# Sending the samples' memory queries to all partitions by DMA, in place of products with the identity

## The chip, the core and the metric

One core of a Trainium2 chip runs the whole kernel in one launch. The metric is the device time in microseconds, the median of several executions. Engines: TensorE (PE) for products, VectorE (DVE), ScalarE (ACT), GpSimd (POOL), and SyncE (SP), which here only issues loads. Data lies in 128 partitions of on-chip memory (SBUF); products land in banks of PSUM.

## The reference

A decoder layer runs on two inputs at once: a prompt of 512 tokens and 8 samples of one token each. The part that matters is the memory attention:

```python
def mem_attend(h, mk, mv, w_xq, w_xo):
    q = (h @ w_xq).reshape(B, T, MEM_HEADS, MEM_HEAD_DIM)             # 4 heads of 256
    s = jnp.einsum('bthd,bmhd->bhtm', q, mk).astype(jnp.float32) * MEM_SCALE
    p = jax.nn.softmax(s, -1).astype(mv.dtype)
    o = jnp.einsum('bhtm,bmhd->bthd', p, mv).reshape(B, T, MEM_HEADS * MEM_HEAD_DIM)
    return o @ w_xo
```

For the prompt, keys and values are projected from 256 memory tokens (`mem @ w_mk`, `mem @ w_mv`). For the samples they come from a cache: each of the 8 samples has its own 256 keys and 256 values in every head, 1 MB of keys and 1 MB of values per sample.

## The kernel before

All activations are held transposed (features on partitions, 520 tokens along the row, in two halves of 260). Every large product is made from float32 values split in two parts, high and low: three matmuls (L1944 high by high, L1945, L1946) for each 128 x 128 block. A weight slot is loaded into `wraw` (two buffers), ScalarE writes its high part `whi` (L912), VectorE its low part `wlo` (L1394). The load queue may send slot s when VectorE has split slot s-2 (`load_w`, wait on `w_lo`), and ScalarE may overwrite a `whi` when TensorE is done with the slot three back.

The order of work is written out by hand on each engine, and each engine waits for semaphores. PSUM has a ring of seven banks: the list `bank_order` says in which order results take them.

Around the change the order is this. The query projection `xq` has 8 tiles (m = 0..7), two for each head. After m = 2, 4, 6 and 7, `query_rows(h)` turns the 8 sample columns of head h (kept in `qcs`) into 8 rows (L2320), and ScalarE scales them into `q_nat` (L928), 8 partitions x 256. A sample's scores need its 256 keys, which lie in `kv_slot` as 128 partitions x 2 keys; so the query of a sample and head has to stand in all 128 partitions. `spread(g)` makes that with the identity: a full float32 product of `q_nat` with one broadcast column of `ident` (L2329) fills half a bank for each (head, sample) pair. VectorE then multiplies and sums it against the two keys of each partition (`scores_of`, L1738, two products a pair), into `Sc`. The 32 pairs come in nine groups `SPREADS`, g0 to g8, each in two halves. A half is one bank.

Groups g0 to g3 follow xq tiles 3, 5, 6 and 7 on TensorE and VectorE. Groups g4 to g7 follow the first four tiles of the memory key projection (`key_tile(j)`, slots S_MEM to S_MEM+3, "mm"), on VectorE each behind the split of slot S_MEM+j+2. Then come the prompt's scores of head 0 (`mem_scores(0)`), their maxima on VectorE (L1785), g8, the maximum over the samples' scores (L1808), and on TensorE the first value tile (`value_tile(0)`, slots S_MEM+4 and S_MEM+5). The maximum goes through TensorE once (L2435), becomes a diagonal (L1815) and is spread by one product (L2439). Key tile 4 (slot S_MEM+6) stands ahead of that product, key tile 5 (S_MEM+7) behind it.

The cached keys and values share eight 1 MB slots. Keys 0 to 6 are loaded before and during the projections, key 7 when xq tile 7 is done. Values take over slots whose keys are spent: `K_SLOT` and `V_SLOT` give the slots, and the load queue waits for the score groups.

Of the kernel before, what the change touches and what calls it, by code (L numbers as in the profile page):

```python
# [81 lines left out]
SPREADS = [[[(0, 0), (0, 1)], [(0, 2)]], [[(1, 0), (1, 1)], [(1, 2)]],  # L82
# [4 lines left out]

K_SLOT, V_SLOT = [0, 1, 2, 3, 4, 5, 6, 7], [3, 5, 4, 6, 2, 7, 2, 7]
# [17 lines left out]
def bank_order():  # L106
# [37 lines left out]
    def spread(g):  # L144
        return [("qb", g, i) for i in (0, 1)]

# [9 lines left out]
    for m in range(KD):  # L156
        o += [("xq", m, f) for f in (0, 1)]
        if m == 0:
            o += [("ssq", "nx")]
        if m in (2, 4, 6):  # L160
            o += [("qt", m // 2 - 1)]
        if m in (3, 5, 6, 7):
            o += spread((3, 5, 6, 7).index(m))
    o += [("qt", 3)]
    for j in range(4):
        o += [("mm", j)] + spread(4 + j)
    o += mem_scores(0) + [("mn", 0)] + spread(8) + [("mv", 0), ("cmxt",), ("mm", 4), ("cmxb",), ("mm", 5)]
# [113 lines left out]
def build(nc, a, consts, outs):  # L281
# [4 lines left out]
    with ctx:  # L286
# [125 lines left out]
        q_by = q_diag[:, 0:NK * NB * G16].rearrange("p (x i h) -> p x i h", i=P // SQ, h=NH)  # L412
# [49 lines left out]
        q_nat = at("q_nat", [D], F32, o_rstd)  # L462
        prod = at("prod", [MD], F32, o_tmp)
# [8 lines left out]
        qcs = keep("qcs", [KD, NB])  # L472

# [67 lines left out]
        qcs_set = sem("qcs_set")  # L541
        stored = sem("stored")
# [148 lines left out]

        def cached(eng, n):
# [18 lines left out]
        def _(sp):  # L711
# [88 lines left out]
        def _(gp):  # L800
# [96 lines left out]
            gp.memset(Pv_pad[:, :], 0.0).then_inc(vpad_set, 1)  # L897
            squares("nf", "xo2", KD, lambda c: xT[:, c, :])
# [3 lines left out]
        def _(act):  # L902
# [1683 lines left out]
```

## Time and profile before

| | |
|---|---|
| three timed runs | 903.75 us median (900.0 to 905.21) |
| the profiled execution | 899.05 us, span 897.3 us |
| TensorE busy | 828.3 us (92%) |
| VectorE busy | 484.9 us (54%) |
| ScalarE busy | 327.2 us (36%) |
| GpSimd busy | 103.1 us (11%) |
| mean granted TensorE clock | 0.958 |
| moved by DMA | 102.57 MB, 114 GB/s over the span |

The profile gives each instruction with its line, what it writes and reads, and what ended the idle time of its engine ahead of it. Times are microseconds from the start of the span. "Clock" is the granted TensorE clock as a share of 2.4 GHz; 0.50 is 1.2 GHz. A matmul's duration in the timeline reaches into the next one, since they are pipelined; the distance between starts is what one costs. In L2329 one product is recorded twice.

### The profile page before, as it was taken

What the parts mean: (1) busy time and instruction counts of PE and PEld (TensorE: products, weight loads), DVE (VectorE), ACT (ScalarE), POOL (GpSimd) and SP (SyncE); (2) the same over time, 40 slices, a digit from 0 to 9 for tenths busy, and PEclk for the clock granted to TensorE, in tenths of its full rate; (3) what the DMA queues carried; (4) which work ended last, traced back from release to release, by engine and by line L of the source; (5) the groups of instructions that cost most, each with busy time, mean ns of one, the idle gap of its engine ahead of it and who ended that gap; (6) DMA issues with size and microseconds to landing.
All of it is one profiled execution on the core that took longest, in us unless ns stands there. A gap on an engine that the chain in (4) does not pass through costs nothing.

```text
span 897.3 us, 16200 instructions
## 1 busy us (share of the span) xinstructions
PE 828.3 (92%) x6599; PEld 788.0 (88%) x6599; DVE 484.9 (54%) x1055; ACT 327.2 (36%) x714; POOL 103.1 (11%) x143
## 2 busy tenths in 40 slices
PE   5989989877899999789999899999999999999994
PEld 4979978733799998689799899999999999999994
DVE  5577556584354457665555475555555555222322
ACT  5314676510342323355533343333333333112312
POOL 0366104020134000000035100000000000000000
PEclk8999998879799999889999999999999999999998
DMA  7412337040723714573623233333332232332312
GB/s 218 122 48 81 87 96 293 2 175 1 257 71 101 253 48 142 207 258 115 219 72 95 71 94 95 94 95 95 95 92 86 87 91 88 109 110 83 88 42 95
DMA packets 133792, 102.57 MB, mean 114 GB/s; under 512 B 8567, under 2 KB 127280, under 8 KB 130639
## 3 DMA queue, kind: packets, MB, share of 16 engines
q1 hardware_dynamic: 128231, 87.17, 31.7%
q0 software_dynamic: 1792, 10.49, 3.0%
q10 hardware_dynamic: 3696, 3.88, 1.3%
q8 instruction: 52, 0.85, 0.4%
q14 instruction: 21, 0.17, 0.1%
HBM read 96.59 MB, written 5.17 MB: 113 GB/s over the span
## 4 chain that ended last, share of the span: by engine, by line
PE 77%; DVE 6%; ACT 4%; DMA 3%; issue 2%; SPq 0%; ACTq 0%; DVEq 0%
PE ps L1944 23%; PE ps L1946 23%; PE ps L1945 23%; DMA wraw<-in_w_mk_dram 2%; DVE turned_c L1667 1%; PE ps L2281 1%; PE ps L2421 1%; DVE prod L1738 1%; DMA kv_slot<-in_cache_mem_v_dram 1%; PE ps L2376 1%; PE ps L2377 1%; PE ps L2378 1%; PE ps L2329 1%; DVE turned_r L1668 1%; PE ps L2253 0%
## 5 line engine op out<-in xcount | busy, mean ns | idle before, releaser
L1944 PE MATMUL ps<-B_hi,whi 128*128 128x260 f32 x992 | 283.4, 286 | 9.9 <-DVE wlo L1394 4.3
L1946 PE MATMUL ps<-B_hi,wlo 128*128 128x260 f32 x992 | 281.4, 284 | 0.0
L1945 PE MATMUL ps<-B_lo,whi 128*128 128x260 f32 x992 | 281.2, 283 | 0.0
L1394 DVE TENSOR_TENSOR wlo<-wraw,whi 128x512 fp32r<-128x512 f32 (+1 forms) x250 | 170.2, 723 | 167.1 <-ACT whi L912 164.8
L912 ACT ACTIVATE whi<-wraw 128x512 fp32r<-128x512 f32 (+1 forms) x250 | 140.3, 610 | 201.8 <-PE ps L1946 159.2
L1944 PEld LDWEIGHTS ps<-B_hi,whi 128*128 128x128 f32 x992 | 187.9, 189 | 11.9 <-issue 9.3
L1946 PEld LDWEIGHTS ps<-B_hi,wlo 128*128 128x128 f32 x992 | 188.3, 190 | 0.0
L1945 PEld LDWEIGHTS ps<-B_lo,whi 128*128 128x128 f32 x992 | 188.1, 190 | 0.1
L1945 PE MATMUL ps<-h_lo,whi 128*128 128x260 f32 x352 | 99.7, 283 | 0.0
L1946 PE MATMUL ps<-h_hi,wlo 128*128 128x260 f32 x352 | 99.4, 282 | 0.0
L1944 PE MATMUL ps<-h_hi,whi 128*128 128x260 f32 x352 | 99.4, 282 | 0.0
L1944 PE MATMUL ps<-A_hi,whi 128*128 128x260 f32 x264 | 76.2, 289 | 1.6 <-DVE A_lo L1394 1.2
L1946 PE MATMUL ps<-A_hi,wlo 128*128 128x260 f32 x264 | 75.7, 287 | 0.0
L1945 PE MATMUL ps<-A_lo,whi 128*128 128x260 f32 x264 | 75.6, 286 | 0.0
L1944 PEld LDWEIGHTS ps<-h_hi,whi 128*128 128x128 f32 x352 | 66.3, 188 | 0.0
L1946 PEld LDWEIGHTS ps<-h_hi,wlo 128*128 128x128 f32 x352 | 66.3, 188 | 0.0
L1945 PEld LDWEIGHTS ps<-h_lo,whi 128*128 128x128 f32 x352 | 66.2, 188 | 0.0
L1944 PEld LDWEIGHTS ps<-A_hi,whi 128*128 128x128 f32 x264 | 51.1, 193 | 2.1 <-DVE A_lo L1394 1.6
L1945 PEld LDWEIGHTS ps<-A_lo,whi 128*128 128x128 f32 x264 | 51.0, 193 | 0.1
L1946 PEld LDWEIGHTS ps<-A_hi,wlo 128*128 128x128 f32 x264 | 50.9, 193 | 0.0
L1424 DVE TENSOR_TENSOR xT<-ps,xT 128x260 f32<-128x260 f32 x48 | 20.4, 426 | 55.8 <-PE ps L1946 54.7
L918 ACT ACTIVATE h_hi<-hv 128x260 fp32r<-128x260 f32 x44 | 18.6, 422 | 71.9 <-DVE hv L1876 71.9
(405 smaller groups left out, 1286.4 us busy)
## 6 DMA issues: line engine op xcount, KB each, us to landing
wraw<-in_w_gate_dram SPq DMA_DIRECT2D x22, 512.0 KB, 3.8
wraw<-in_w_up_dram SPq DMA_DIRECT2D x22, 512.0 KB, 3.8
kv_slot<-in_cache_mem_k_dram SPq DMA_DIRECT2D x8, 1024.0 KB, 9.3
kv_slot<-in_cache_mem_v_dram SPq DMA_DIRECT2D x8, 1024.0 KB, 6.9
wraw<-in_w_down_dram SPq DMA_DIRECT2D x16, 512.0 KB, 4.0
wraw<-in_w_in_dram SPq DMA_DIRECT2D x9, 512.0 KB, 4.1
wraw<-in_w_out_dram SPq DMA_DIRECT2D x8, 512.0 KB, 4.1
wraw<-in_w_xq_dram SPq DMA_DIRECT2D x8, 512.0 KB, 5.2
```

The source lines that it names most:

```text
L912: act.activation(whi[:, s % SPL, c0:c1], wraw[:, s % RAW, c0:c1], ACT.Copy).then_inc(w_hi, 1)
L918: act.activation(dst, src, ACT.Copy, scale=scale).then_inc(hi, 1)
L1394: return dve.tensor_tensor(dst, src, high.bitcast(F32), ALU.subtract)
L1424: ins = dve.tensor_tensor(xT[:, m, c0:c1], b[:, 0:TH], xT[:, m, c0:c1], ALU.add)
L1667: dve.transpose(turned_c[:, b % 2].rearrange("p j k t -> p (j k t)"), past_c[b].rearrange("p j r -> p (j r)"))
L1668: value(("turned", b), dve.transpose(turned_r[:, b % 2].rearrange("p j k t -> p (j k t)"), past_r[b].rearrange("p j r -> p (j r)")))
L1738: ins = dve.tensor_tensor_reduce(prod[:, :], keys[:, m2, h * MD:(h + 1) * MD], q[:, n * MD:(n + 1) * MD], 1.0, 0.0, ALU.mult, ALU.add, Sc[ ...
L1944: pe.matmul(dst, left[0], right[0], start=first, stop=False)
L1945: pe.matmul(dst, left[0], right[1], start=False, stop=False)
L1946: return pe.matmul(dst, left[1], right[0], start=False, stop=last)
L2281: ins = pe.matmul(accO[strip, 0:KVL], P_pad[:, c:c + SQ], past_c[b][:, j, :], start=(b == 0 and 0 < j < 4), stop=(b == NB - 1 and j >= 4), ...
L2329: ins = pe.matmul(b[:, n * MD:(n + 1) * MD], ident[0:NB, sample:sample + 1].to_broadcast([NB, P]), q_nat[0:NB, h * MD:(h + 1) * MD], start ...
```

## The change

The queries reach the 128 partitions by DMA. ScalarE still scales the 8 rows of a head into `q_nat`, which now has two buffers; it then waits for its own result and stores the rows (8 x 1 KB) into a tensor `q_rows` in device memory. GpSimd issues, for each half group, one load that reads one or two rows and writes them to all 128 partitions, 128 KB for each pair, into one of four buffers `q_by`. It waits for the store of the heads involved and, from the fifth half on, for VectorE to have spent the half four places back (`q_spent`). VectorE's products read `q_by` in place of PSUM. The `spread` products and their 18 places in the ring of banks are gone.

The order of the groups changes too. They follow xq tiles 4 to 7 (before 3, 5, 6, 7), and their members are others: g4 now has three pairs and g7 three, g5 and g6 four. Keys 4 and 5 swap slots, and the load queue waits for other groups at other places.

```diff
-SPREADS = [[[(0, 0), (0, 1)], [(0, 2)]], [[(1, 0), (1, 1)], [(1, 2)]],
-           [[(0, 3), (0, 4)], [(0, 5), (0, 6)]], [[(2, 0), (2, 1)], [(2, 2)]],
...
+SPREADS = [[[(0, 0), (0, 1)], [(0, 2)]], [[(0, 3), (0, 4)], [(0, 5), (0, 6)]],
+           [[(1, 0), (1, 1)], [(1, 2)]], [[(1, 3), (1, 4)], [(1, 5), (1, 6)]],
+           [[(2, 0), (2, 1)], [(2, 2)]], [[(2, 3), (2, 4)], [(3, 3), (3, 4)]],
+           [[(2, 5), (2, 6)], [(3, 5), (3, 6)]], [[(3, 0), (3, 1)], [(3, 2)]],
            [[(0, 7), (1, 7)], [(2, 7), (3, 7)]]]
-K_SLOT, V_SLOT = [0, 1, 2, 3, 4, 5, 6, 7], [3, 5, 4, 6, 2, 7, 2, 7]
+QBUF = 4
+K_SLOT, V_SLOT = [0, 1, 2, 3, 5, 4, 6, 7], [3, 5, 4, 6, 2, 7, 2, 7]
...
+        q_by = [at(f"q_by{i}", [2, MD], F32, o) for i, o in enumerate((o_rstd + 2048, o_rstd + 4096, o_tmp, take(2048)))]
+        q_rows = nc.dram_tensor("q_rows", [NH, NB, MD], F32, kind="Internal").ap()
...
             for i in range(2, len(MEM_TILES) + 2):
                 load_w(S_MEM + i)
-                if i == 5:
-                    freed(sp, ("qb", 7, 1))
-                if 5 <= i < 9:
-                    load_kv(NB + i - 5)
-                if i == 10:
-                    load_kv(NB + 4)
-                    freed(sp, ("qb", 8, 1))
-                if i == 11:
-                    load_kv(NB + 5)
+                if i in (4, 6, 8, 9):
+                    spent(sp, {4: 5, 6: 6, 8: 7, 9: 8}[i], 1)
+                for b in {4: (0,), 5: (1,), 6: (2,), 7: (3,), 9: (4,), 10: (5,)}.get(i, ()):
+                    load_kv(NB + b)
...
+            for g, halves in enumerate(SPREADS):
+                for i, members in enumerate(halves):
+                    n = 2 * g + i
+                    for h, _ in members:
+                        gp.wait_ge(q_out[h], 16)
+                    if n >= QBUF:
+                        gp.wait_ge(q_spent, n - QBUF + 1)
...
+                    gp.dma_start(q_by[n % QBUF][:, 0:len(members), :], rows.rearrange("h b d -> (h b) d").unsqueeze(0)
+                                 .to_broadcast([P, len(members), MD])).then_inc(q_in[n % QBUF], 16)
...
+                freed(act, ("qt", h))
+                act.dma_start(q_rows[h], q_nat[0:NB, h % 2, :]).then_inc(q_out[h], 16)
...
                 for i, members in enumerate(SPREADS[g]):
-                    q = full(dve, ("qb", g, i))
+                    slot_ = (2 * g + i) % QBUF
+                    dve.wait_ge(q_in[slot_], 16 * ((2 * g + i) // QBUF + 1))
...
-                                prod[:, :], keys[:, m2, h * MD:(h + 1) * MD], q[:, n * MD:(n + 1) * MD],
+                                prod[:, :], keys[:, m2, h * MD:(h + 1) * MD], q_by[slot_][:, n, :],
...
-                if m in (3, 5, 6, 7):
-                    scores_of((3, 5, 6, 7).index(m))
+                if m >= 4:
+                    scores_of(m - 4)
...
-            def spread(g):
...
-                        ins = pe.matmul(b[:, n * MD:(n + 1) * MD], ident[0:NB, sample:sample + 1].to_broadcast([NB, P]),
-                                        q_nat[0:NB, h * MD:(h + 1) * MD], start=True, stop=True)
...
             for j in range(4):
                 key_tile(j)
-                spread(4 + j)
             mem_scores(0)
             key_rows(0)
-            spread(8)
```

On TensorE, at the end of the last xq tile, these instructions stood before (the last product of the tile, group g3 of three pairs, the turn of head 3, the first products of key tile 0):

```order
L1946 MATMUL ps<-B_hi,wlo 128x260
L2329 MATMUL ps<-q_nat,ident 128x256 [waits bank_free6,lo]
L2329 MATMUL ps<-q_nat,ident 128x256 [waits bank_free6]
L2329 MATMUL ps<-q_nat,ident 128x256 [waits bank_free6,lo]
L2320 MATMUL ps<-ident,qcs 8x128 [waits qcs_set,bank_free6]
L2320 MATMUL ps<-ident,qcs 8x128
L1944 MATMUL ps<-mT_hi,whi 128x256 [waits bank_free0,w_lo,lo]
```

and these stand there now:

```order
L1963 MATMUL ps<-B_hi,wlo 128x260
L2337 MATMUL ps<-ident,qcs 8x128 [waits qcs_set,lo]
L2337 MATMUL ps<-ident,qcs 8x128
L1961 MATMUL ps<-mT_hi,whi 128x256 [waits lo,w_lo]
L1962 MATMUL ps<-mT_lo,whi 128x256
```

The three products of the group are gone, and with them the waits for their banks; the same holds after xq tiles 3, 5 and 6, after key tiles 0 to 3 and after the key rows of head 0.

On the load queue (SP), from the load of key 7 on, before (`in_w_mk` are key tiles, `in_w_mv` halves of a value tile, `in_cache_mem_v` cached values; `bank_free4` there is the release of group g7):

```order
L754 DMA kv_slot7_180<-in_cache_mem_k_dram 128x2048 [waits bank_full3]
L719 DMA wraw_50<-in_w_mk_dram 128x8x128 [waits w_lo] x2
L719 DMA wraw_50<-in_w_mv_dram 128x4x256 [waits w_lo] x2
L754 DMA kv_slot3_176<-in_cache_mem_v_dram 128x2048 [waits bank_free4]
L719 DMA wraw_50<-in_w_mk_dram 128x8x128 [waits w_lo]
L754 DMA kv_slot5_178<-in_cache_mem_v_dram 128x2048
L719 DMA wraw_50<-in_w_mk_dram 128x8x128 [waits w_lo]
L754 DMA kv_slot4_177<-in_cache_mem_v_dram 128x2048
L719 DMA wraw_50<-in_w_mv_dram 128x4x256 [waits w_lo]
L754 DMA kv_slot6_179<-in_cache_mem_v_dram 128x2048
```

and now (the first `q_spent` is for group g5, the second for g6):

```order
L759 DMA kv_slot7_180<-in_cache_mem_k_dram 128x2048 [waits bank_full4]
L724 DMA wraw_50<-in_w_mk_dram 128x8x128 [waits w_lo] x2
L724 DMA wraw_50<-in_w_mv_dram 128x4x256 [waits w_lo]
L759 DMA kv_slot3_176<-in_cache_mem_v_dram 128x2048 [waits q_spent]
L724 DMA wraw_50<-in_w_mv_dram 128x4x256 [waits w_lo]
L759 DMA kv_slot5_178<-in_cache_mem_v_dram 128x2048
L724 DMA wraw_50<-in_w_mk_dram 128x8x128 [waits w_lo]
L759 DMA kv_slot4_177<-in_cache_mem_v_dram 128x2048 [waits q_spent]
L724 DMA wraw_50<-in_w_mk_dram 128x8x128 [waits w_lo]
L759 DMA kv_slot6_179<-in_cache_mem_v_dram 128x2048
```

The first cached values moved one weight load forward: they and their wait for scores now stand ahead of the second half of value tile 0 (slot S_MEM+5). The wait itself is for g5, where it was for g7.

## Rows read from the trace of the kernel before

**Rows 1.** Busy PE, PEld, DVE, ACT, POOL (records) in stretches, clock, DMA share, GB/s.
```profile
310.94:371.92 60.98, 60.98 (x435) 55.10 (x434) 43.41 (x162) 20.29 (x46) 0.00 (x0) 1.00 0.29 88
341.45:344.45 3.00, 3.00 (x26) 2.86 (x24) 2.14 (x10) 0.47 (x1) 0.00 (x0) 1.00 0.89 343
377.45:382.09 4.64, 4.64 (x24) 4.44 (x24) 1.15 (x2) 1.81 (x4) 0.00 (x0) 0.63 1.08 397
382.09:385.14 3.05, 0.00 (x1) 0.03 (x1) 2.71 (x7) 1.18 (x3) 0.00 (x0) 0.87 1.01 398
385.67:390.96 5.29, 5.29 (x25) 5.29 (x25) 2.55 (x6) 1.85 (x5) 0.00 (x0) 0.50 0.91 316
```

**Rows 2.** One line, L2329: min/median/max ns, first and last start us.
```profile
L2329 PE MATMUL ps<-q_nat,ident x64: 374/374/477, 310.9 to 365.9; 8*128 8x256 f32 x64
```

**Rows 3.** Timeline of TensorE: start us, us, instruction; two half groups, the matmul behind.
```profile
310.94 1.56 PE L2329 MATMUL ps<-q_nat,ident 8*128 8x256 f32 x6
312.43 0.39 PE L1944 MATMUL ps<-B_hi,whi 128*128 128x260 f32 x1
...
331.96 1.99 PE L2329 MATMUL ps<-q_nat,ident 8*128 8x256 f32 x8
333.88 0.39 PE L1944 MATMUL ps<-B_hi,whi 128*128 128x260 f32 x1
```

**Rows 4.** Timeline of the load queue (SP): start us, us spent issuing, transfer.
```profile
339.93 0.34 SPq L754 DMA_DIRECT2D kv_slot<-in_cache_mem_k_dram  x1
...
348.81 5.61 SPq L719 DMA_DIRECT2D wraw<-in_w_mv_dram  x2
...
367.54 0.34 SPq L754 DMA_DIRECT2D kv_slot<-in_cache_mem_v_dram  x1
367.93 0.42 SPq L719 DMA_DIRECT2D wraw<-in_w_mk_dram  x1
```

**Rows 5.** Timeline of ScalarE: first use of two weight loads, idle time before.
```profile
346.75 1.16 ACT L912 ACTIVATE whi<-wraw 128x512 fp32r<-128x512 f32 x2 [4.49 <-DMA wraw<-in_w_mk_dram]
...
375.44 1.15 ACT L912 ACTIVATE whi<-wraw 128x512 fp32r<-128x512 f32 x2 [3.46 <-DMA wraw<-in_w_mk_dram]
```

**Rows 6.** Chain of waits in order of time: start us, us, what.
```profile
369.02 11.24 DMA wraw<-in_w_mk_dram
```

**Rows 7.** Timeline of VectorE: splits of w2 to w5, maxima and end of scores, splits w6, w7.
```profile
347.48 1.30 DVE L1394 TENSOR_TENSOR wlo<-wraw,whi 128x512 fp32r<-128x512 f32 x2 [3.75 <-ACT whi L912]
...
352.73 1.29 DVE L1394 TENSOR_TENSOR wlo<-wraw,whi 128x512 fp32r<-128x512 f32 x2
...
357.98 1.29 DVE L1394 TENSOR_TENSOR wlo<-wraw,whi 128x512 fp32r<-128x512 f32 x2
...
362.30 1.29 DVE L1394 TENSOR_TENSOR wlo<-wraw,whi 128x512 fp32r<-128x512 f32 x2
...
367.54 1.42 DVE L1785 TENSOR_REDUCE cstat<-ps 128x2 f32<-128x512 f32 x2
...
372.82 0.22 DVE L1808 TENSOR_REDUCE cols<-Sc 128x32 f32<-128x64 f32 x1
...
376.10 1.29 DVE L1394 TENSOR_TENSOR wlo<-wraw,whi 128x512 fp32r<-128x512 f32 x2 [3.06 <-ACT whi L912]
...
380.94 1.29 DVE L1394 TENSOR_TENSOR wlo<-wraw,whi 128x512 fp32r<-128x512 f32 x2 [3.55 <-ACT whi L912]
```

**Rows 8.** VectorE by tile: min/median/max ns, first and last start us; operands, shapes.
```profile
L1738 DVE CUSTOM_DVE_ANT_0 prod<-kv_slot,ps x64: 413/420/424, 312.1 to 372.4; 128x256 f32<-128x256 f32 x64
...
L1394 DVE TENSOR_TENSOR mk_lo<-kv_T,mk_hi x8: 417/422/428, 348.7 to 412.5; 128x256 fp32r<-128x256 f32 x8
...
L1394 DVE TENSOR_TENSOR kl<-kr,kk x4: 744/1190/1287, 58.4 to 62.1; 64x260 fp32r<-64x260 f32 x2, 64x252 fp32r<-64x252 f32 x2
```

**Rows 9.** POOL's own issue in ns; time to landing of the cached key and value loads.
```profile
L892 POOL DMA_INDIRECT past_c<-in_cache_kv_latent_dram,row_ids x8: 940/943/1173, 136.6 to 187.0; - x8
...
DMA to landing us min/median/max: 4.9/8.2/13.0
```

More of the change, by code:

```diff
@@ L143, in bank_order @@
             o += [("mt", k) for k in range(4)]
-    def spread(g):
-        return [("qb", g, i) for i in (0, 1)]
     def mem_scores(h):
@@ L541, in build @@
         qcs_set = sem("qcs_set")
+        q_out = [sem(f"q_out{h}") for h in range(NH)]
+        q_in = [sem(f"q_in{i}") for i in range(QBUF)]
+        q_spent = sem("q_spent")
         stored = sem("stored")
@@ L690, in build, with spent @@
             kv_count.append(seen[i])
+        def spent(eng, g, i):
+            eng.wait_ge(q_spent, 2 * g + i + 1)
         def cached(eng, n):
@@ L897, in _ @@
             gp.memset(Pv_pad[:, :], 0.0).then_inc(vpad_set, 1)
+            full(gp, ("ssq", "nx"))
+            for g, halves in enumerate(SPREADS):
[5 more added lines that the diff above has]
+                        gp.wait_ge(q_spent, n - QBUF + 1)
+                    (h0, b0_), (h1, b1_) = members[0], members[-1]
+                    rows = q_rows[h0:h0 + 1, b0_:b1_ + 1, :] if h0 == h1 else q_rows[h0:h1 + 1, b0_:b0_ + 1, :]
+                    gp.dma_start(q_by[n % QBUF][:, 0:len(members), :], rows.rearrange("h b d -> (h b) d").unsqueeze(0)
+                                 .to_broadcast([P, len(members), MD])).then_inc(q_in[n % QBUF], 16)
             squares("nf", "xo2", KD, lambda c: xT[:, c, :])
@@ L1151, in _ @@
                 group = slice(SQ * i, SQ * (i + 1))
-                ins = act.activation(q_by[group, :, i, :], x[group, 0:NK * NB * NH].rearrange("p (x h) -> p x h", h=NH), ACT.Copy)
+                ins = act.activation(q_diag_by[group, :, i, :], x[group, 0:NK * NB * NH].rearrange("p (x h) -> p x h", h=NH), ACT.Copy)
                 if i < P // SQ - 1:
@@ L1250, in value_tile @@
                 if h == 0:
-                    freed(act, ("qb", 6, 1))
+                    spent(act, 7, 1)
                 else:
@@ L1276, in turned @@
                     if h == 0 and mb == 0:
-                        freed(act, ("qb", 6, 1))
+                        spent(act, 7, 1)
                     high(("cpt", h, mb), PTc_hi[:, mb, :], b)
@@ L1742, in scores_of @@
                                 step(ins)
-                    frees(ins, ("qb", g, i))
-                    freed(dve, ("qb", g, i))
+                    ins.then_inc(q_spent, 1)
+                    spent(dve, g, i)
             for m in range(KD):
@@ L2321, in query_rows @@
                 filled(ins, ("qt", h))
-            def spread(g):
-                for i, members in enumerate(SPREADS[g]):
-                    b = out(("qb", g, i))
-                    for n, (h, sample) in enumerate(members):
-                        freed(pe, ("qt", h))
-                        ins = pe.matmul(b[:, n * MD:(n + 1) * MD], ident[0:NB, sample:sample + 1].to_broadcast([NB, P]),
-                                        q_nat[0:NB, h * MD:(h + 1) * MD], start=True, stop=True)
-                    filled(ins, ("qb", g, i))
             for m in range(KD):
@@ L2346, in _ @@
                     query_rows(m // 2 - 1)
-                if m in (3, 5, 6, 7):
-                    spread((3, 5, 6, 7).index(m))
             query_rows(3)
```

16 lines of the change are left out of this document (8 added, 8 removed), and 2 rows, old and new, of the table SPREADS.

## The prediction

> **What bounds the kernel now.** I began with the granted clock and the engine table, which say that TensorE is busy in 92% of the span, and then cut the memory attention into stretches. From 310.94 to 371.92 us TensorE is never idle [rows 1]. Part of that work is what the change deletes: the 64 recorded passes of L2329, the spreading products [rows 2]. The order of TensorE shows that they stand in its way: a half group of three samples pushes the next matmul from 310.94 to 312.43, a group of four from 331.96 to 333.88 [rows 3], that is 1.49 and 1.92 us. Over nine groups (four of three samples, five of four) this is 4 x 1.49 + 5 x 1.92 = 15.6 us.
>
> That is not yet the gain. The chain of waits from 347 to 385 us does not run through those products. It runs through VectorE's score products, the load queue that waits for them, and a weight load of 11.24 us [rows 6]. VectorE has no idle time from 347.48 until its last score at 372.82 [rows 7]. TensorE then stands still: mk tile 4 begins at 377.45 and runs at a mean granted clock of 0.63, nothing runs from 382.09 to 385.14, and mk tile 5 takes 5.29 us at clock 0.50 (1.2 GHz), where mk tile 0 took 3.00 at full clock [rows 1]. So there are three limits in a row: TensorE to the end of the query projection, VectorE through the scores, late loads behind them. I price each in turn.
>
> Names: w2 to w7 are the loads of the memory projection's slots S_MEM+2 to S_MEM+7 (w2, w3 and w6, w7 for mk tiles 2, 3 and 4, 5; w4, w5 the halves of value tile 0). v0 to v5 are the loads of cached values. g4 to g8 are the last five score groups.
>
> **Step 1: TensorE up to the end of the query projection.** Groups g0, g1 and g2 of before stand ahead of xq tile 7: 1.49 + 1.49 + 1.92 = 4.90 us. With them gone, tile 7 ends at 339.93 - 4.90 = 335.0. Nothing else is late there: in the new order an xq tile with four samples costs VectorE what a key tile with four does, 5.25 us, and one low part more (0.42 [rows 8]), less than the 6.0 us of TensorE (48 matmuls, 24 in 3.00 [rows 1]). (The 5.25: a split and low part with four samples takes 352.73 - 347.48 = 5.25, one with three 362.30 - 357.98 = 4.32 [rows 7]; one sample, two products, is 0.93.) The remaining 10.7 us of products lie beside VectorE's work, and I count them as nothing.
>
> **Step 2: w2 still waits for tile 7.** The queue sends key load 7 at 339.93 when tile 7 ends, then w2 and w3 [rows 4]. w2 is in at 346.75, and VectorE splits it at 347.48 [rows 5, 7], 7.55 us behind the end of tile 7. This is not touched, so the split comes at 342.6. But now two broadcasts (256 KB each, g5's) share the engines. At the 343 GB/s of that stretch [rows 1] one of them costs 0.75 us; I add 0.7 for one and get 343.3.
>
> **Step 3: VectorE's chain, and a load that was put behind a wait.** From the split of w2: g4 now has three samples (4.32), g5 has four (5.25), so g5 is spent at 352.9. Here the order of the load queue hurts. Before, w5 left with the pair at 348.81, ahead of the wait for the scores [rows 4]. Now v0 stands ahead of w5, and v0 waits for g5. What this looks like was seen later in the old trace: v0 at 367.54, w6 at 367.93, and w6 in use by ScalarE at 375.44 [rows 4, 5], 7.9 us after v0. Add 0.9 us for g7's broadcasts (384 KB at about 0.4 MB per us [rows 1]): w5 is in at 361.7 and its VectorE split begins 0.66 later (376.10 - 375.44), at 362.4. VectorE is ready at 352.9 + 5.25 = 358.1, so it waits 4.3 us. Then split and g7 (4.32) to 366.7; the maxima of score tile 0 and g8, as before 372.82 - 367.54 = 5.28 [rows 7], to 372.0. Before this was 372.82. Nearly the whole lead is used up at this point.
>
> **Step 4: the loads behind the scores are early.** Before, w6 and w7 were ordered only after 367.54 and came late: VectorE waited 3.06 and 3.55 us for them [rows 7]. Now w6 leaves at about 354 and w7 at about 364, as soon as their buffers are split, and w7 even with its old 11.24 us is needed only at 372.8 plus ScalarE's exponentials; with four 1 MB loads spread over 15 us instead of crowded into 3 I take it to be in by 370. mk tile 4 starts 1.35 us after the split of w6 (377.45 - 376.10), at 372.0 + 0.2 + 1.35 = 373.55, 3.9 us earlier. I leave it its 4.64 us, since TensorE idles about as long ahead of it: end 378.2. VectorE's path to the diagonal (second split to release of TensorE 385.14 - 380.94 = 4.2, plus 1.2 for the first split) would be ready at 377.6, so the idle 3.05 us vanish. mk tile 5 starts 0.53 later, at 378.7 against 385.67: 7.0 us earlier. Since TensorE now runs through, as it had from 377.45 when its clock came back, I take tile 5 at 3.07 instead of 5.29 us: 2.2 more.
>
> **The sum.** 7.0 + 2.2 = 9.2 us, from 391 us on a pure shift: the remaining stages have the same work and loads with the same distances. The profiled execution took 899.05 us with a span of 897.3; less 9.2 it is 889.9. The three timed runs have a median of 903.75, 4.7 above it, so I forecast 894.5 for a median.
>
> **Costs that no row shows.** The round trip (8 KB to device memory, then a broadcast to 128 partitions): the nearest rows are cached loads of 1 MB, which land in 4.9 to 13.0 us [rows 9]; POOL's own issue takes 0.94 [rows 9]. A broadcast smaller by four to eight times should be near the low end, 5 us with the issue. What it may take: buffers turn after four halves; g6's first half is ordered when g4's first is spent (346.7) and needed at 354.4, 7.7 us later, and if it is late it eats only into the 4.3 us wait for w5. g7 and g8 have 12 us. So up to about 12 us the trip costs nothing. The four stores cost ScalarE half a microsecond each, beside tiles for which it waits. POOL has nothing behind them but the squares for the last norm, far later.
>
> The product from SBUF instead of PSUM: 420 ns with one operand in PSUM; a 256-column subtraction with both operands in SBUF takes 422 [rows 8]. I take it as unchanged, with 0.05 us per product (1.8 us over 36) to either side. The Trainium skill, "VectorE: DVE Perf Modes", section on the TRN2 errata, gives a fixed part of 120 cycles from PSUM and 58 from SBUF, which would make each product 65 ns shorter and the last 36 of them 2.3 us; these rows show no such difference, so the sum goes without it.
>
> Two SBUF operands can also collide with POOL: the four kl subtractions took 1.19 us in the median instead of 0.42 [rows 8], which I put down to POOL's tensor work beside them. If an issue of 0.94 us stopped VectorE wholly, the two that fall ahead of g5's end would cost 1.9 us; the lower bound is zero, and I take zero, the issue being no tensor work. The Trainium skill, "SBUF — State Buffer", section "Who interferes with whom", says that two-input operations contend only with GpSimd's reads of SBUF, and infers that writing descriptors needs the write side; the kl rows fit the first, no row here tests the second.
>
> **Rivals.** (A) The forecast, 7 to 11.5 us gained. (B) w5 is not late: v0 goes out slowly enough or bandwidth suffices, as for w5 before, whose split at 357.98 waited for nothing [rows 7]. The 4.3 us come back; mk tile 4 could start at 369.3 and tile 5 at 374.4: gain 13.5, time 890.2. For it speaks that the engines are idle at 358 us in the old trace; against it, that the same order of loads gave 7.9 us there. (C) The gain is mostly lost: broadcasts of 12 to 13 us, or the freed time is handed to later waits (TensorE waits once for the v7 load near 443 us, and values could crowd weights again), or tile 5 stays at 1.2 GHz and w6 or w7 come late too, 11.24 us after their turn. Gain 0 to 4.5, time about 901. (D) The broadcast replaces the product as the bound. Every fourth half waits for a trip of L: from g0's first half spent (319.5) four trips lead to g8: g8 begins at 319.5 + 4L + 3 x 1.86. The gain is gone when g8's end comes at 381.2, which is L = 13.1 us, just over the slowest load of this trace; at L = 15 the kernel is 4 x 1.9 = 7.6 us slower, 911.4. It would need each small broadcast, through POOL's queue, to be slower than the slowest 1 MB load. Against: those loads queued behind each other.
>
> **How the numbers follow.** A 0.58, B 0.12, C 0.20, D 0.10. A difference of 0.5% (4.5 us) is about what a measurement of this kernel can tell from none. Faster: A, B and 0.06 of C, 0.76. Same: the rest of C, 0.14. Slower: D, 0.10. The timed runs spread over 5 us, so the range must be wider than A's own (892 to 897): from just beyond B, 888.5, into C at 901.5; what lies outside is D, a part of C and a little above B.
>
> **What would show it.** Right: no TensorE record in L2329's place; tile 7 ends near 335; VectorE idles some 4 us for a w_mv weight near 358 us, ahead of g7; no idle time on it for a q_by broadcast; the last score near 372, almost unmoved; mk tile 5 near 379 at clock 1.00, and from there the old trace shifted by about 9. Step 3 is wrong if VectorE does not wait for w5 (then B), or waits for q_in (C, D); step 4 if mk tile 4 waits for w_mk as before. The forecast is wrong as a whole if the stage ends earlier and the kernel does not.

## The result and the profile after

The changed kernel took 893.68 us in the median of five runs (892.82 to 894.52), the kernel before 903.75 beside it: ratio 0.9893, 95% interval 0.9867 to 0.9919. That is 10.1 us less, where 9.2 were forecast. The profiled execution took 892.82 us, span 890.9.

The two traces cannot be laid on each other by their absolute times. These rows are the first matmul of xq tile 0 and the first product with w_xo, of before, of the changed kernel, and of the changed kernel run again later, unedited:

```profile
286.45 0.36 PE L1944 MATMUL ps<-B_hi,whi 128*128 128x260 f32 x1 [0.96 <-issue]
450.26 0.39 PE L1944 MATMUL ps<-A_hi,whi 128*128 128x260 f32 x1 [0.64 <-DVE A_lo L1394]
```
```profile
290.88 0.36 PE L1961 MATMUL ps<-B_hi,whi 128*128 128x260 f32 x1 [0.96 <-issue]
443.95 0.39 PE L1961 MATMUL ps<-A_hi,whi 128*128 128x260 f32 x1 [0.64 <-DVE A_lo L1410]
```
```profile
283.45 0.36 PE L1961 MATMUL ps<-B_hi,whi 128*128 128x260 f32 x1 [0.96 <-issue]
437.28 0.39 PE L1961 MATMUL ps<-A_hi,whi 128*128 128x260 f32 x1 [0.64 <-DVE A_lo L1410]
```

The reader is to see that the stage is entered at 290.88 us in one trace and 283.45 in the other of the same program. Every time below is therefore counted from xq tile 0. "Forecast" is the prediction's own number less 286.45.

| from xq tile 0, us | before | forecast | after | after, again |
|---|---|---|---|---|
| end of xq tile 7 | 53.5 | 48.6 | 48.0 | 48.0 |
| split of w2 | 61.0 | 56.9 | 55.5 | 55.6 |
| split of w5 | 75.9 | 76.0 | 74.3 | 74.5 |
| end of the scores | 86.4 | 85.6 | 83.9 | 84.1 |
| mk tile 4 begins | 91.0 | 87.1 | 85.6 | 85.8 |
| mk tile 5 begins | 99.2 | 92.3 | 91.4 | 91.7 |
| prompt scores of head 1 | 104.5 | 95.3 | 94.3 | 94.7 |
| first product with w_xo ("the stage") | 163.8 | 154.6 | 153.1 | 153.8 |
| end of the span | 610.9 | 601.7 | 600.0 | 599.2 |

VectorE after, the splits of w2, w5, w6, w7 and the end of the scores, which answer to [rows 7]:

```profile
346.42 1.29 DVE L1410 TENSOR_TENSOR wlo<-wraw,whi 128x512 fp32r<-128x512 f32 x2 [2.93 <-ACT whi L924]
...
365.13 1.29 DVE L1410 TENSOR_TENSOR wlo<-wraw,whi 128x512 fp32r<-128x512 f32 x2 [3.84 <-ACT whi L924]
...
374.78 0.22 DVE L1825 TENSOR_REDUCE cols<-Sc 128x32 f32<-128x64 f32 x1
...
375.10 1.29 DVE L1410 TENSOR_TENSOR wlo<-wraw,whi 128x512 fp32r<-128x512 f32 x2
...
377.76 1.29 DVE L1410 TENSOR_TENSOR wlo<-wraw,whi 128x512 fp32r<-128x512 f32 x2 [1.36 <-ACT whi L924]
```

The wait for w5 is there, 3.84 us. The two waits of 3.06 and 3.55 us for w6 and w7 have become none and 1.36. The load queue after, which answers to [rows 4]:

```profile
338.89 0.34 SPq L759 DMA_DIRECT2D kv_slot<-in_cache_mem_k_dram  x1
...
356.04 0.34 SPq L759 DMA_DIRECT2D kv_slot<-in_cache_mem_v_dram  x1
356.81 0.37 SPq L724 DMA_DIRECT2D wraw<-in_w_mv_dram  x1
...
366.45 0.37 SPq L724 DMA_DIRECT2D wraw<-in_w_mk_dram  x1
```

v0 leaves at 356.04, w5 at 356.81, and w7 only at 366.45, when w5's split at 365.13 has freed its buffer. Before, w5 had left ahead of every cached value and had come into use 3.57 us later (these two lines are of before):

```profile
354.05 0.37 SPq L719 DMA_DIRECT2D wraw<-in_w_mv_dram  x1
357.62 1.15 ACT L912 ACTIVATE whi<-wraw 128x512 fp32r<-128x512 f32 x2 [2.35 <-DMA wraw<-in_w_mv_dram]
```

Now ScalarE uses w5 7.59 us behind its issue and 8.36 us behind v0, and w7 10.65 us behind its issue:

```profile
364.40 1.15 ACT L924 ACTIVATE whi<-wraw 128x512 fp32r<-128x512 f32 x2 [10.53 <-DMA wraw<-in_w_mv_dram]
...
377.10 1.15 ACT L924 ACTIVATE whi<-wraw 128x512 fp32r<-128x512 f32 x2 [1.50 <-DMA wraw<-in_w_mk_dram]
```

mk tiles 4 and 5 (the columns are those of [rows 1]); the last column but two is the clock:

```profile
376.45:381.70 5.25, 5.25 (x24) 5.04 (x24) 3.60 (x7) 2.26 (x5) 0.00 (x0) 0.54 0.99 357
382.26:385.35 3.09, 3.09 (x27) 3.09 (x27) 2.21 (x6) 2.21 (x6) 0.00 (x0) 1.00 0.95 380
```

The 3.05 us of idleness between them are now 0.25 (the product of the diagonal starts at 381.96, its input is made from 381.58 to 381.81). Tile 5 runs at full clock, tile 4 at nearly half. Ahead of tile 4 TensorE had stood idle for 5.13, 3.53 and 0.94 us, together 9.60, where before it had stood for 1.27 and 4.00:

```profile
366.48 0.58 PE L2381 MATMUL ps<-whi,mT_hi 128*128 128x256 f32 x1 [5.13 <-DVE wlo L1410]
...
375.14 0.37 PE L2438 MATMUL ps<-ident,cols 128*32 128x128 f32 x1 [3.53 <-DVE cols L1825]
```

The broadcasts and the products that read them:

```profile
L1755 DVE CUSTOM_DVE_ANT_0 prod<-kv_slot,q_by x64: 414/424/428, 322.1 to 374.3; 128x256 f32<-128x256 f32 x64
L908 POOL DMA_DIRECT2D q_by<-q_rows x18: 537/539/726, 312.6 to 361.9; - x18
...
who waited for it (us, times):
busy tenths in 40 slices 0000000000000046500000000000000000000000
DMA to landing us min/median/max: 3.1/3.9/9.2
```

Nobody waited for a broadcast: the line "who waited for it" has nothing under it, and VectorE has no idle time of any label ahead of a product that reads `q_by`.

### The profile page after: what moved, and what is told of

The parts are those of the page before. It is cut to its first block, busy times and chain, and to the rows that moved or that the text cites. A ratio compares the mean times of both kernels' runs of the same rounds, so it can differ in the third digit from the quotient of the medians.

```text
span 890.9 us, 16093 instructions
## 1 busy us (share of the span) xinstructions
PE 813.9 (91%) x6535; PEld 776.5 (87%) x6535; DVE 484.5 (54%) x1055; ACT 326.9 (37%) x714; POOL 113.2 (13%) x161
## 4 chain that ended last, share of the span: by engine, by line
PE 77%; DVE 6%; DMA 4%; ACT 3%; issue 2%; another core or an unknown queue 0%; SPq 0%; ACTq 0%; DVEq 0%
PE ps L1961 23%; PE ps L1963 23%; PE ps L1962 23%; DMA wraw<-in_w_mk_dram 2%; DVE turned_c L1683 2%; PE ps L2298 1%; DMA wraw<-in_w_mv_dram 1%; PE ps L2426 1%; PE ps L2381 1%; PE ps L2383 1%; PE ps L2382 1%; DMA kv_slot<-in_cache_mem_v_dram 1%; DVE turned_r L1684 1%; PE ps L2247 1%
## 5 line engine op out<-in xcount | busy, mean ns | idle before, releaser
L1962 PEld LDWEIGHTS ps<-h_lo,whi 128*128 128x128 f32 x352 | 66.2, 188 | 0.0
```

The source lines that it names most:

```text
L1962: pe.matmul(dst, left[0], right[1], start=False, stop=False)
```

## The experiments

All later runs were made beside new runs of the kernel before, which took 896.4 to 897.0 us in the median there, 0.8% less than in the first comparison. So ratios are compared, not times, and beside the ratios the stage (from xq tile 0 to the first product with w_xo), which came to 153.1 and 153.8 us in the two traces of one kernel, while the entry into it ranged from 282.7 to 290.9 us over all fourteen traces. "Rest" is from that product to the end of the span: the same work in every kernel, and yet it ranges over 3.3 us, and over 1.6 us in the two traces of one kernel. Stage and rest come from one trace of each kernel (two of the changed one), so a difference in the stage of less than about 1 us shows nothing, and the ratios, with their intervals of about 2 us to either side, show only the large ones.

| kernel | ratio (95%) | stage | rest |
|---|---|---|---|
| before | 1 | 163.8 | 447.0 |
| changed, first | 0.9893 (0.9867 to 0.9919) | 153.1 | 446.9 |
| changed, again | 0.9878 (0.9853 to 0.9902) | 153.8 | 445.3 |
| DMA queries, old groups and loads | 0.9978 (0.9960 to 0.9996) | 161.3 | 448.5 |
| products, new groups and loads | 0.9919 (0.9892 to 0.9945) | 155.8 | 448.5 |
| w5 ahead of v0 | 0.9892 (0.9872 to 0.9912) | 151.6 | 448.4 |
| w2 and w3 ahead of key 7 | 0.9878 (0.9857 to 0.9900) | 151.8 | 446.9 |
| both | 0.9845 (0.9819 to 0.9870) | 149.8 | 446.9 |
| both, g8 apart | 0.9868 (0.9845 to 0.9890) | 149.4 | 447.0 |
| the same, w7 ahead of v2 and v3 | 0.9877 (0.9853 to 0.9900) | 150.4 | 447.0 |
| the same, TensorE filled | 0.9860 (0.9840 to 0.9879) | 149.2 | 446.6 |
| DMA queries, old groups and loads, g5's broadcasts held | 0.9971 (0.9952 to 0.9991) | 161.3 | 448.6 |
| DMA queries, old groups, w2 and w3 ahead | 0.9912 (0.9892 to 0.9932) | 156.4 | 447.0 |
| changed, two buffers | 0.9982 (0.9962 to 1.0001) | 163.9 | 447.0 |

**The changed kernel again.**

> The changed kernel itself, unedited, on the chip of the runs beside it, as their common measure and to see what of its profile is its own. Theory: where it enters the memory attention (first matmul of xq tile 0 at 290.88 us in the first profile, 286.45 in that of before) is chance, since nothing ahead of it differs; the entry moves by some microseconds here, and the stretch from there to the prompt scores of head 1 stays at 94.3 us (before 104.5). The ratio to before is again 0.987 to 0.992. Rival: the entry is again 4 us late, so something of the change acts upstream.

Measured: entry at 283.45 us, 3.0 earlier than before where it had been 4.4 later; to the scores of head 1 94.7; ratio 0.9878. The theory holds: the entry moves from run to run of one program, and the change has no part in it.

**One half alone: the DMA.** The changed kernel with before's `SPREADS`, slots and load order (one of its places):

```diff
-                if m >= 4:
-                    scores_of(m - 4)
+                if m in (3, 5, 6, 7):
+                    scores_of((3, 5, 6, 7).index(m))
```

> One half of the change alone: the queries go by DMA, but groups, members, slots and load order are those of before (groups behind xq tiles 3, 5, 6, 7; v0 behind w5 and g7; four buffers). Theory (the two halves add up): the 4.9 us of products ahead of the end of xq tile 7 go, all behind it shifts by that, w5 is not late, but w6 and w7 come late as before (VectorE waits about 3 us for each, mk tile 5 at half clock): 4.5 to 5 us gained, 899 us (ratio 0.9945). Rival (the new load order carries the whole gain, and the freed TensorE time goes into waits for the same loads): 0 to 1 us gained, 903. A second rival, that this half carries all of it: 894.

**The other half alone: groups and loads.** The kernel before with the new `SPREADS`, slots and load order; the products stay (one of its places):

```diff
-                if m in (3, 5, 6, 7):
-                    spread((3, 5, 6, 7).index(m))
+                if m >= 4:
+                    spread(m - 4)
```

> The other half alone: the spreading products stay on TensorE, but groups, members, slots and load order are those of the changed kernel. Theory (the halves add up): tile 7 ends as late as before (4.9 us of products ahead of it), w5 comes late behind v0 (VectorE idle about 4 us), w6 and w7 are in early, mk tile 5 at full clock: 4 to 5 us gained, 899 us (ratio 0.995). Rival: without the freed time the late w5 eats up what w6 and w7 give, and the time is that of before, 902 to 904, or worse.

The DMA half shortens the stage by 2.5 us, the order half by 8.0; together 10.5, where the changed kernel has 10.7 and 10.0. They do add up, but not as expected (about 5 each). The ratios say the same within their intervals: 2.0 and 7.3 us. The products removed, 15.6 us of TensorE's time, are worth 2.5 us. The order half holds three things, the groups, the slots of the keys and the places of the loads; they were not tried apart.

Where the DMA half loses its lead, VectorE shows at the split of w2:

```profile
341.62 1.29 DVE L1415 TENSOR_TENSOR wlo<-wraw,whi 128x512 fp32r<-128x512 f32 x2 [6.39 <-ACT whi L929]
```

xq tile 7 ended at 330.69 us, 48.0 after tile 0, 5.5 sooner than before. But w2 is split 10.9 us behind it, not 7.55, so 2.1 us of the lead are left. (Ahead of that, with g1 still behind xq tile 5, VectorE also stood 2.05 us for a broadcast at 322.04, which it does not in the changed kernel; TensorE did not wait for it.) Around the tile's end GpSimd issued broadcasts (start, us, instruction):

```profile
327.35 1.06 POOL L913 DMA_DIRECT2D q_by<-q_rows  x2 [7.95 <-DMA q_rows<-q_nat]
329.18 0.54 POOL L913 DMA_DIRECT2D q_by<-q_rows  x1 [0.76 <-DVE Sc L1760]
331.04 0.54 POOL L913 DMA_DIRECT2D q_by<-q_rows  x1 [1.33 <-DVE Sc L1760]
334.85 0.54 POOL L913 DMA_DIRECT2D q_by<-q_rows  x1 [3.27 <-DVE Sc L1760]
335.79 0.54 POOL L913 DMA_DIRECT2D q_by<-q_rows  x1 [0.40 <-issue]
```

I took the last four, 1 MB, for the cause and held back the last two:

```diff
                         gp.wait_ge(q_out[h], 16)
+                    if n == 10:
+                        gp.wait_ge(w_loaded[(S_MEM + 2) % RAW], landed[S_MEM + 2])
                     if n >= QBUF:
                         gp.wait_ge(q_spent, n - QBUF + 1)
```

> The half change with DMA queries and the old groups and loads, and GpSimd holds the broadcasts of g5 until w2 has landed. In that half change 1 MB of broadcasts (g4 and g5) was ordered between 329 and 336 us, around the end of xq tile 7 at 330.7, and w2 came into use 10.2 us after the end of tile 7 where the changed kernel took 6.8; it gained 2.3 us of the 5.5 that the deleted products give there. Theory (the broadcasts crowd w2): with half of them held back w2 is in use 8.2 to 9 us after tile 7's end, and the stretch from xq tile 0 to the scores of head 1 shortens by 1 to 2 us. Rival (something else delays w2, key load 7 or the store of the query rows): still 10 us, nothing gained.

The split came 10.35 us behind the tile in place of 10.93, the first use of w2 9.62 in place of 10.20, and the stage did not move. The expectation failed: the two broadcasts ordered behind w2 cost it about 0.6 us, in one trace of each. And VectorE then stood 2.00 us for the last half of g8, whose broadcast was ordered at 358.23 and landed some 10 us later, where without the hold that wait was 0.57:

```profile
368.38 0.43 DVE L1762 CUSTOM_DVE_ANT_0 prod<-kv_slot,q_by 128x256 f32<-128x256 f32 x1 [2.00 <-issue]
```

What delayed w2 by the rest, the broadcasts ordered ahead of key 7 or something else, was not separated. Whether the wait for w2 is on the path of this half was then tried directly:

```diff
+            load_w(S_MEM + 2)
+            load_w(S_MEM + 3)
             full(sp, ("xq", KD - 1, 1))
             load_kv(7)
-            for i in range(2, len(MEM_TILES) + 2):
+            for i in range(4, len(MEM_TILES) + 2):
```

> The half change with DMA queries and the old groups and loads, with one edit: w2 and w3 go out ahead of key load 7, as tried on the changed kernel. Measured by the stretch from xq tile 0 to the first product with w_xo (before 163.8 us, this half change 161.3, the other half 155.8, the changed kernel 153.1 and 153.8). Theory (in this half VectorE's 6.39 us for w2 ate what the deleted products gave at the end of tile 7): the wait goes and the stretch falls by 4 to 6.4 us, to 155 to 157. Rival (the late w6 and w7 behind the scores hold the stage, w2 is covered): it stays above 160.

156.4 us, as expected: the 6.39 us wait is gone, and the stage is 7.5 us shorter than before instead of 2.5. The waits for w6 and w7 were left as they were (2.90 and 3.45). This is not the worth of the products with w2 repaired: the kernel before, in which VectorE stands 3.75 us for w2 [rows 7], was not run with w2 ahead.

**Why the order half gives more.** In it mk tile 4 took 3.10 us at full clock; in the changed kernel 5.25 at 0.54:

```profile
375.41:378.51 3.10, 3.10 (x24) 2.89 (x24) 2.96 (x5) 1.15 (x3) 0.00 (x0) 1.00 0.60 176
```

TensorE's longest pause ahead of that tile was 1.55 us there, against 5.13 and 3.53. The products between key tiles fill the waits; that such filling raises the clock is shown on another kernel below. Counting: mk tile 4 begins 1.6 us sooner than before, takes 1.5 less (4.64), the pause behind it is 0.79 in place of 3.05, and tile 5 runs at full clock: with that, 8.0 by the scores of head 1 (96.5 against 104.5). Against the changed kernel, tile 4 begins 3.8 us later (89.4 against 85.6), and 2.15 of that come back in the tile itself. VectorE's wait for w5 was shorter too, 2.23 us in place of 3.84:

```profile
364.11 1.29 DVE L1389 TENSOR_TENSOR wlo<-wraw,whi 128x512 fp32r<-128x512 f32 x2 [2.23 <-ACT whi L907]
```

**The two waits of the changed kernel.** First w5, step 3 of the prediction (rival B's condition, brought about):

```diff
-                if i in (4, 6, 8, 9):
-                    spent(sp, {4: 5, 6: 6, 8: 7, 9: 8}[i], 1)
-                for b in {4: (0,), 5: (1,), 6: (2,), 7: (3,), 9: (4,), 10: (5,)}.get(i, ()):
+                if i == 6:
+                    load_kv(NB + 1)
+                if i in (5, 6, 8, 9):
+                    spent(sp, {5: 5, 6: 6, 8: 7, 9: 8}[i], 1)
+                for b in {5: (0,), 6: (2,), 7: (3,), 9: (4,), 10: (5,)}.get(i, ()):
```

> The changed kernel with one edit: w5, the second weight load of value tile 0, goes out ahead of the wait for group g5 and of v0 (order now w4, w5, [g5] v0, w6, v1, [g6] v2, w7). Theory (step 3: the late w5 is on the path): in the changed kernel VectorE idles 3.84 us for it and TensorE 5.13. That VectorE wait falls under 0.5 us, the last score comes 3 to 4 us sooner after xq tile 0, and the kernel takes about 890 us, 3.5 below the changed kernel (ratio to before 0.985). Rival (the stage is held by the next loads anyway): the wait moves to w6 or w7, which now stand behind v0 and v1, and the time stays at 893 to 894 (0.989).

VectorE in this kernel, the split of w5 and group g8:

```profile
356.46 1.29 DVE L1412 TENSOR_TENSOR wlo<-wraw,whi 128x512 fp32r<-128x512 f32 x2
...
363.18 0.43 DVE L1757 CUSTOM_DVE_ANT_0 prod<-kv_slot,q_by 128x256 f32<-128x256 f32 x1 [0.75 <-DMA q_by<-q_rows]
...
367.16 0.42 DVE L1757 CUSTOM_DVE_ANT_0 prod<-kv_slot,q_by 128x256 f32<-128x256 f32 x1 [2.14 <-issue]
```

The split waits for nothing, 3.65 us sooner after xq tile 0 than in the changed kernel. But now VectorE waits twice for a broadcast. The second wait is labelled "issue"; the last broadcast says what it is. It was issued at 356.99, behind v0, w6, v1 and v2, and the landing times of the last two broadcasts (window 355 to 358 us) are:

```profile
DMA to landing us min/median/max: 8.0/9.0/10.1
```

356.99 + 10.1 = 367.1. Of 3.84 us 2.9 turned into that wait. Such a broadcast now had 7.3 and 8.0 us from its issue until VectorE was ready for it; in the changed kernel, with 3.84 us of waiting in front, g8's two had about 11. The end of the scores came 0.7 us sooner, the stage is 1.8 shorter than the mean of the changed kernel's two, and of that the ratio shows nothing (the rest of this trace is 448.4). Neither theory was right: the rival named w6 and w7.

Second w2, step 2 (the diff is the one above):

> The changed kernel with one edit: w2 and w3 go out ahead of the wait for the end of xq tile 7 and of key load 7; everything else keeps its order. Theory (step 2: the 7.55 us from the end of tile 7 to the split of w2 stand on the path of VectorE): the split of w2 comes within 2 us of the end of tile 7 in place of 7.56, the waits of TensorE for w2 and w3 (1.93 and 1.35 us) go, all of the chain behind shifts by 5 to 6.5 us, the kernel takes about 888 us (ratio 0.982). Rival (the chain is held by v0 and w5 or by key 7, which land when they did): gain under 1.5 us, 892 to 894.

```profile
340.11 1.29 DVE L1412 TENSOR_TENSOR wlo<-wraw,whi 128x512 fp32r<-128x512 f32 x2
...
360.00 1.29 DVE L1412 TENSOR_TENSOR wlo<-wraw,whi 128x512 fp32r<-128x512 f32 x2 [4.00 <-ACT whi L926]
```

The split comes 4.7 us behind tile 7 (335.44), not within 2: VectorE itself is busy with g3 until then. Of the 7.55 us only the 2.93 of waiting were to be had. The expectation of 5 to 6.5 us failed; VectorE also stood 0.93 us for a broadcast of g4. The stage is 1.7 us shorter.

> The changed kernel with both edits tried apart: w2 and w3 ahead of key load 7, and w5 ahead of v0. Alone each took 1.4 to 1.8 us off the stretch from xq tile 0 to the prompt scores of head 1 (94.31 us in the changed kernel, 92.54 and 92.91). Theory X (with both gone, the broadcasts of g8, which land behind the cached values, are the wait, as in the first edit, where VectorE stood 0.75 and 2.14 us for them): these waits grow to 3 to 5 us together, the stretch is 91 to 92.5 us, kernel 2 to 3 us below the changed kernel. Theory Y (the gains add): no such growth, the stretch is 89 to 91 us, kernel 4 to 5 us below.

Stage 149.8, 3.7 us under the mean of the changed kernel's two, which is about the sum of the two gains (1.8 and 1.7); 91.2 us to the scores of head 1. VectorE waited 0.56 and 2.92 us for g8's broadcasts. These waits and the 91.2 us lie in theory X, at its lower end; that the gains add is what theory Y said. The two theories were too close for one trace to part them. The median is 1.0 us below the changed kernel's, less than either said. The ratio is the lowest of all, but its interval overlaps those of most others.

**g8's broadcasts apart.** They get two buffers of their own, and wait for the end of the last xq tile in place of a spent half. The part that orders them:

```diff
-            for g, halves in enumerate(SPREADS):
-                for i, members in enumerate(halves):
-                    n = 2 * g + i
+            for n in list(range(14)) + [16, 17, 14, 15]:
+                for members in (SPREADS[n // 2][n % 2],):
```

> As the last one, and the two broadcasts of g8 have buffers of their own and are ordered ahead of those of g7, so they go out before the cached values. Theory X (g8's broadcasts are what held the last): VectorE waits for no q_by, the last score comes 3 to 5 us sooner than in the kernel with both edits, the stretch is 87.5 to 90 us and the kernel 2 to 4 us below that one, the fastest of all: ratio to before 0.981 to 0.985. Rival: w6 and w7, ordered behind the same values, or the exponentials and value tile, take over as the wait; under 1 us gained.

```profile
355.24 0.43 DVE L1763 CUSTOM_DVE_ANT_0 prod<-kv_slot,q_by 128x256 f32<-128x256 f32 x1 [1.79 <-DMA q_by<-q_rows]
...
366.67 1.29 DVE L1418 TENSOR_TENSOR wlo<-wraw,whi 128x512 fp32r<-128x512 f32 x2 [1.70 <-ACT whi L932]
```

The wait moved to g7, now ordered behind them, and w7 is late by 1.70. The end of the scores came 1.2 us sooner (79.8 after xq tile 0), the stage is 0.4 shorter, within the spread of one kernel's traces. The rival was right.

**w7, and TensorE's clock.**

```diff
-                if i in (5, 6, 8, 9):
-                    spent(sp, {5: 5, 6: 6, 8: 7, 9: 8}[i], 1)
-                for b in {5: (0,), 6: (2,), 7: (3,), 9: (4,), 10: (5,)}.get(i, ()):
+                if i in (5, 7, 8, 9):
+                    spent(sp, {5: 5, 7: 6, 8: 7, 9: 8}[i], 1)
+                for b in {5: (0,), 7: (2, 3), 9: (4,), 10: (5,)}.get(i, ()):
```

> The kernel with w2, w3 and w5 early and g8's own buffers, with w7 also ahead of v2 and v3. There w7 took 11.9 us from issue to use and VectorE stood 1.70 us for it; TensorE ran mk tile 4 at half clock (5.49 us) after 7.45 us of idleness, and ended it as late as the diagonal came. Theory: the wait for w7 goes, but mk tile 4 at half clock holds the place: 0.3 to 0.8 us gained of 1.7, stretch 148.6 to 149.2 (149.4 there). Rival: the full 1.7, 147.7.

The wait for w7 went, but the stage is 150.4. This time w5 was late by 3.00 us: ordered at the same point as in the kernel before it in the table, it came into use 70.8 us after xq tile 0 in place of 66.2, with the same transfers in the same order ahead of it, and a later weight load made VectorE wait 2.96 us. So this one trace cannot price w7's place.

Then TensorE's pause was filled in this kernel:

```diff
             b = out(("cmxt",))
+            for _ in range(48):
+                pe.matmul(b[:, 0:NMEM], mT_hi[:, 0, 0:P], mT_hi[:, 1, :], start=True, stop=True)
             after(("cmx",))
```

> As the last one, with 48 products of 128 x 256 that compute nothing used, put on TensorE between the first value tile and the turn of the maximum, into the bank that the turn overwrites. They fill some 6 of the 7.5 us in which TensorE stood there. Theory (the idle time costs the clock, and the clock now costs time): mk tile 4 takes 3.1 us in place of 5.5, the diagonal is then the bound, and the stretch shortens by 1 to 2 us against the kernel without them, to 147 to 148. Rival (the diagonal's chain or later waits hold it anyway): mk tile 4 at full clock but the stretch the same within 0.4 us.

mk tile 4, in the kernel without and with the filling:

```profile
367.02:372.36 5.34, 5.33 (x25) 5.20 (x25) 3.57 (x7) 1.15 (x3) 0.00 (x0) 0.53 0.94 302
```
```profile
368.31:371.38 3.07, 3.07 (x28) 2.94 (x25) 2.28 (x5) 0.00 (x0) 0.00 (x0) 1.00 0.92 315
```

The filling began at 362.24, later than meant since w5 was late here too (2.06 us), and ran to 368.28, 2.7 us past the point at which the turn of the maximum could have begun. Two things are shown. Without the idle time the clock is full: 1.00 from 364 us on, still inside the filling, and in mk tile 4. And the clock is a bound on tile 5 in the kernel without: there the diagonal is made from 370.53 us, and the product that spreads it starts at 372.29, behind tile 4; with the filling the two times are 370.43 and 371.31.

What the filling is worth is not shown. mk tile 5 began 86.5 us after xq tile 0, 2.0 sooner than without, but 1.1 of these were there at the end of the scores (80.1 against 81.2), ahead of the turn, with w5 less late (2.06 us against 3.00). That leaves 0.9 us, which by the first product with w_xo is gone again: the stage is 1.2 shorter in all. 149.2 us misses the expected 147 to 148, and the intervals of the two ratios overlap.

**Two buffers.** `QBUF = 2` in place of 4.

> The changed kernel with two buffers for the spread queries in place of four, so that each broadcast is ordered only when the half two back is spent. It prices the trip. Rival D of the prediction has a law for it: time between halves is the trip. The trips took 3.9 us in the median and 9.2 at worst from the issue, plus 0.54 for the issue; VectorE has 3.5 us of other work in between (the other half 1.86, split and low part 1.65). Theory: VectorE waits for q_by 1 to 1.5 us in each quiet group and up to 5 behind the cached values, in part in place of the 3.84 us for w5; the stretch grows by 4 to 8 us to 157.5 to 161.5, the kernel with it. Rival (the trip is covered even so): under 2 us.

```profile
361.48 0.42 DVE L1755 CUSTOM_DVE_ANT_0 prod<-kv_slot,q_by 128x256 f32<-128x256 f32 x1 [3.06 <-issue]
366.13 0.42 DVE L1755 CUSTOM_DVE_ANT_0 prod<-kv_slot,q_by 128x256 f32<-128x256 f32 x1 [1.13 <-DMA q_by<-q_rows]
370.40 0.43 DVE L1755 CUSTOM_DVE_ANT_0 prod<-kv_slot,q_by 128x256 f32<-128x256 f32 x1 [2.44 <-issue]
375.99 0.42 DVE L1755 CUSTOM_DVE_ANT_0 prod<-kv_slot,q_by 128x256 f32<-128x256 f32 x1 [3.04 <-DMA q_by<-q_rows]
379.61 0.43 DVE L1755 CUSTOM_DVE_ANT_0 prod<-kv_slot,q_by 128x256 f32<-128x256 f32 x1 [1.79 <-issue]
```

With two more, of 1.33 and 0.72 us, these waits make 13.5 us. They replace the 3.84 for w5, and w2 is split 1.5 us later: 11.2, and the end of the scores is 11.4 later. (Waits labelled "issue" are counted as waits for a broadcast, as in the kernel with w5 first.) The stage is 163.9 us and the ratio 0.9982: the whole gain of the change hangs on the second pair of buffers. I had expected 4 to 8 us and a stage of 161.5 at most; the direction and the mechanism (rival D's) hold, the size, 10.4 us, lies above the range.

## Why the prediction was right, and where it was not

The forecast was 894.5 us and the result 893.7; the sum of 9.2 us stands against 10.2 by the scores of head 1 (9.8 in the second trace) and 10.1 in the timed medians. Part of that closeness is luck: steps 1 and 2 came out better than forecast and two terms of step 4 worse, and the absolute time rests on an offset that no row explains.

**What bounds the kernel.** "Three limits in a row" (TensorE, VectorE with the loads, late loads) is what the traces show; the third, the late w6 and w7, was never repaired alone. The offset of 4.7 us between the profiled execution and the median of before was added without a cause. The entry into the stage moves by that much from run to run, but the timed runs have no traces, so that it was this is not shown; and the same kernel had 896.4 to 897.0 us in all later runs. That it fitted is luck.

**Step 1** held: 5.5 us where 4.9 were forecast. The start-to-start readings of [rows 3] leave out how the group's own start and the matmul behind it are delayed: around the group at 324.32 us the last matmul of the tile starts at 324.12 and the second one of the next tile at 326.04, 1.92 us where two undisturbed steps take 0.24, so 1.68 for the group and not 1.49. The claim that the other 10.7 us of products cost nothing is borne out too: all 15.6 us together are worth 2.5.

**Step 2** held but for its last term. w2 was split 7.56 us behind tile 7, where the step had 7.55 and 0.7 for broadcasts: the 0.7 did not come. In the changed kernel only one was ordered in that time (342.18), because GpSimd stood for the last store of query rows until 346.72, a store of 8 KB issued at 340.68. The step called the 7.55 us untouched, which was so, but did not see that 4.6 of them were VectorE's own work.

**Step 3** held in its mechanism: 3.84 us of waiting for w5, 4.3 forecast, 8.36 us behind v0 where 8.8 were. Two readings in it and in rival B are wrong and change nothing: the row at 348.81 holds two issues, and w5's is the one at 354.05, still ahead of the wait for the scores; and the split at 357.98 is w4's, w5's is at 362.30 and waited for nothing either. "Nearly the whole lead is used up" was too strong: 2.5 of 5.5 us were left at the end of the scores, since w2 was earlier than forecast.

**Step 4** held in its sum. mk tile 5 came 7.8 us sooner (7.0 forecast) and at full clock. Two terms were off: w7 was not in by 370 but 10.65 us after its issue, and cost 1.36 us; mk tile 4 took 5.25 us, not 4.64, for TensorE had not idled "about as long ahead of it" but 9.60 us instead of 5.27. The earlier start outweighed them.

**The failed step is the one on the trip:** "So up to about 12 us the trip costs nothing". The trip's usual size was well guessed (3.9 us in the median from issue to landing, where 5 were taken with the issue). But the 12 us held the 4.3 us wait for w5. With w5 repaired, trips of 8.0 and 10.1 us behind cached values stopped VectorE for 2.9 us. The trip cost nothing only because the late w5 stood in front of it. For the same reason rival B's price was wrong: it gave w5's 4.3 us back in full, and 1.8 came back in the stage, none in the timed runs.

**The worth of the halves** was wrong too. With the 4.9 us of step 1 put back, the prediction's sum leaves 4.3 us for the order alone; it gained 8.0. Two things in its trace go that way, the shorter wait for w5 (by 1.6 us) and the full clock in mk tile 4 (2.15); the sum has neither.

**The product from SBUF** took 424 ns, 420 from PSUM [rows 8], with a maximum of 428 over 64, so no issue on GpSimd stopped one either. By an estimate from the errata table in the Trainium skill ("VectorE: DVE Perf Modes") it would be 65 ns shorter; measured, it is 4 ns longer. The same section says that its row for SBUF comes out too short; and one operand, the keys, lay in SBUF in both kernels.

Open are why w2 came 3.4 us later in the DMA half, what the groups, the slots and the places of the loads are worth each, what w2 ahead would give the kernel before, and which of the repaired kernels is the fastest. By the stage all four lie 3.0 to 4.2 us under the changed kernel. By the timed runs on its own chip the one with both edits has 884.12 us against 885.12 for the changed one, and their intervals overlap; with two loads moved it is the version I would keep.

## What to carry to other kernels

A stage with three limits in a row gives back little for the removal of one: 15.6 us of TensorE's work was worth 2.5, a new order of groups and loads 8. When a wait is priced, name what stands behind it on the same engine, because that is what takes its place: w5's wait hid the broadcasts, the broadcasts of g8 hid those of g7. And compare traces from a shared event close ahead of the change; the entry into this stage wandered by 8 us over fourteen traces, the stage itself by 0.8 in the two of one kernel.

## What the runs showed that I had not expected

Useless work can be useful: 48 products with no reader raised TensorE's clock from 0.53 to 1.00 in the next tile, 5.34 to 3.07 us, though a gain of the whole kernel is not shown. Small transfers are not quick behind large ones: a store of 8 KB took about 6 us with 2 MB of loads in flight, and a broadcast took 3.1 us at the least in the changed kernel and 10.1 behind cached values in the one with w5 first. One and the same load, w5, came into use 4.6 us apart in two kernels whose orders differ only behind it; the filled kernel, with the second one's order, has it 3.5 us late, and the cause is open.
